# Two edits to the mixture-of-experts stage of a one-core trunk-layer kernel: the first tile's row list and the last tile's result

## What is computed

```python
def hier_moe(h, w_coarse, b_coarse, w_fine, b_fine, w_gate_up, w_down):
    ...
    combine = ((p_grp * grp_oh)[:, :, None] * within[:, None, :]).reshape(-1, N_EXPERTS)
    out = jnp.zeros_like(t)
    for e in range(N_EXPERTS):
        gg, uu = jnp.split(t @ w_gate_up[e], 2, axis=-1)
        out = out + combine[:, e:e + 1] * ((jax.nn.silu(gg) * uu) @ w_down[e])
    return out.reshape(b, s, d)
...
    x = ln_affine(DEEPNORM_ALPHA * x + g2 * y, p['ln2_g'][l], p['ln2_b'][l])
```

## Time and profile before

| | us |
|---|---|
| median of 3 runs | 1366.87 |
| lowest, highest | 1365.56, 1367.5 |
| the profiled execution, its own time | 1364.97 |
| its span, first to last instruction | 1363.0 |
| PE busy | 1237.8 (91%) |
| DVE busy | 954.3 (70%) |
| ACT busy | 657.6 (48%) |
| POOL busy | 202.1 (15%) |
| chain that ended last: PE, DVE, DMA | 79%, 9%, 5% |
| mean granted TensorE clock | 0.953 of full speed |

### The profile page before, as it was taken

The page is one execution under the profiler, slowest core; times in us unless marked ns, Lnnn a source line. Parts: engine busy times, 40 slices in busy tenths (PEclk is TensorE's granted clock), DMA queues, the critical chain, the costliest instruction groups (busy, mean ns, idle before and its releaser), DMA issues.

```text
span 1363.0 us, 20458 instructions
## 1 busy us (share of the span) xinstructions
PE 1237.8 (91%) x6673; PEld 996.4 (73%) x6673; DVE 954.3 (70%) x1716; ACT 657.6 (48%) x1049; POOL 202.1 (15%) x312
## 2 busy tenths in 40 slices
PE   7999999999999899998998999993799999999940
PEld 4777777777888788887876788773588888888830
DVE  5765531839461688888777526788799999999938
ACT  1522222223222677776763213123387788788812
POOL 0023221020232000011111001001011111111101
PEclk9899999999999899999999999995799999999975
DMA  9977664462646678743004534457899999999925
GB/s 349 288 247 239 209 224 171 155 224 83 211 144 182 169 196 217 194 128 90 25 23 132 194 110 140 152 194 266 304 323 366 372 389 385 391 383 379 332 111 146
DMA packets 150338, 301.05 MB, mean 221 GB/s; under 512 B 20380, under 2 KB 31196, under 8 KB 150264
## 3 DMA queue, kind: packets, MB, share of 16 engines
q1 hardware_dynamic: 122424, 232.72, 50.0%
q0 software_dynamic: 21920, 62.13, 14.5%
q10 hardware_dynamic: 5920, 5.24, 1.3%
HBM read 258.71 MB, written 53.38 MB: 229 GB/s over the span
## 4 chain that ended last, share of the span: by engine, by line
PE 79%; DVE 9%; DMA 5%; issue 2%; SPq 2%; ACT 1%; POOL 0%; DVEq 0%; POOLq 0%; ACTq 0%
PE psum_pair L1740 9%; PE psum_pair L1742 8%; PE psum_pair L1741 8%; PE psum_pair L1842 5%; PE psum_pair L2019 5%; PE psum_pair L2021 5%; PE psum_pair L2020 5%; PE psum_pair L1909 4%; PE psum_pair L1911 3%; PE psum_pair L1910 3%; PE psum_pair L1868 3%; PE psum_pair L1853 3%; DMA k_bundle<-k_transposed 3%; PE psum_pair L2034 3%; PE psum_pair L2036 3%; PE psum_pair L2035 3%
## 5 line engine op out<-in xcount | busy, mean ns | idle before, releaser
L1740 PE MATMUL psum_pair<-w_parts,h_hi 128*128 128x512 f32 x520 | 207.4, 399 | 3.0 <-DVE h_lo L1271 3.0
L1742 PE MATMUL psum_pair<-w_parts,h_lo 128*128 128x512 f32 x520 | 203.7, 392 | 0.0
L1741 PE MATMUL psum_pair<-w_parts,h_hi 128*128 128x512 f32 x520 | 203.3, 391 | 0.0
L1121 DVE TENSOR_TENSOR w_parts<-w_raw,w_parts 128x1024 fp32r<-128x1024 f32 x72 | 83.3, 1219 | 92.9 <-ACT w_parts L842 92.3
L982 ACT ACTIVATE p_unnormed<-psum_pair,minus_max 128x640 f32<-128x640 f32 (+1 forms) x160 | 113.3, 711 | 68.6 <-DVE minus_max L1349 67.2
L1842 PE MATMUL psum_pair<-k_bundle,q_bundle 128*128 128x512 f32 (+1 forms) x576 | 124.1, 344 | 14.0 <-ACT p_unnormed L982 9.5
L1349 DVE TENSOR_REDUCE minus_max<-psum_pair 128x1 f32<-128x640 f32 (+1 forms) x160 | 111.8, 715 | 32.3 <-PE psum_pair L1842 29.6
L1740 PEld LDWEIGHTS psum_pair<-w_parts,h_hi 128*128 128x128 f32 x520 | 98.2, 189 | 30.8 <-issue 11.6
L1842 PEld LDWEIGHTS psum_pair<-k_bundle,q_bundle 128*128 128x128 f32 x576 | 89.0, 195 | 34.6 <-issue 20.9
L1742 PEld LDWEIGHTS psum_pair<-w_parts,h_lo 128*128 128x128 f32 x520 | 98.0, 189 | 21.1
L1741 PEld LDWEIGHTS psum_pair<-w_parts,h_hi 128*128 128x128 f32 x520 | 98.3, 189 | 19.5
(11 more groups left out here) (342 smaller groups left out, 2553.5 us busy)
## 6 DMA issues: line engine op xcount, KB each, us to landing
w_raw<-in_w_gate_up SPq DMA_DIRECT2D x76, 512.0 KB, 8.6
w_raw_c<-in_w_gate_up SPq DMA_DIRECT2D x72, 512.0 KB, 9.5
w_raw_b<-in_w_down SPq DMA_DIRECT2D x72, 512.0 KB, 8.6
w_raw<-in_w_in SPq DMA_DIRECT2D x52, 512.0 KB, 8.6
ada_raw<-in_w_ada SPq DMA_DIRECT2D x32, 512.0 KB, 7.6
k_bundle<-k_transposed SPq DMA_DIRECT2D x28, 384.0 KB, 8.5
q_transposed<-turned_staging POOLq DMA_DIRECT2D x40, 256.0 KB, 6.4
ada_raw_early<-in_w_ada SPq DMA_DIRECT2D x16, 512.0 KB, 8.8
```

Of the source, the lines that this page charges most:

```text
L1121: dve.tensor_tensor(w_parts[b % 2][:, 1, c], w_raw[:, c], w_parts[b % 2][:, 0, c].bitcast(F32), ALU.subtract).then_inc(lo_done, 1)
L1740: pe.matmul(out, a_hi, hi, start=kk == 0, stop=False)
L1741: pe.matmul(out, a_hi, lo, start=False, stop=False)
L1742: return pe.matmul(out, a_lo, hi, start=False, stop=kk == KD - 1)
```

## The change

**First tile.** After `positions`, DVE also builds a one-hot matrix `first_tile_pick` for expert 0 alone (a token that chose expert 0 sits in tile 0 at its position), and PE multiplies it by the token numbers (five products with one column, on `psum_pair` 3). DVE turns the result into `rows_wanted`, and the gather of tile 0 starts from that, ahead of the table. The clearing of `expert_in` goes from DVE to ACT. PE turns tile 0 between the two halves of the table's products. ACT rounds tile 0 ahead of the split of the third block of weights; DVE takes its rest after the first chunk of block 0, and writes the table after the four chunks.

**Last tile.** Its result isn't scattered. ACT and DVE take it out of PSUM as a high and a low part, DVE builds a one-hot `last_tile_pick` from the tokens of its slots, and for each tile of tokens PE sums up first choices, second choices (by an fp32 product with the identity) and the last tile's rows (by two products with the one-hot) in PSUM; DVE's `combine` starts from there, without its addition. `moe_over` is given after the store of the last tile but one. Since rows of `pair_rows` that the last tile would have written are then read unwritten, the whole scratch is set to zero beforehand: SP writes a row of zeros to DRAM early on, and after the values of bundles 1 to 5 issues two DMAs each from that row to 128 rows of `pair_rows` (ten of 512 KB, DRAM to DRAM).

```diff
@@ SP
             weights(1)
+            sp.dma_start(zero_scr.rearrange("o (p n) -> (o p) n", p=P), zeros[:]).then_inc(out_cleared, 16)
...
                 load_v(sp, bi, v_in[bi % 2])
+                if bi == 1:
+                    sp.wait_ge(out_cleared, 16 * (TL + 1))
+                if bi <= NT:
+                    for i in (bi - 1, NT + bi - 1):
+                        sp.dma_start(pair_scr[i * P:(i + 1) * P], zero_scr[0:1, :].to_broadcast([P, D])).then_inc(out_cleared, 16)
@@ ACT
             split_hi_moe((0, 0, 0))
+            act.wait_ge(h2_done, NT)
+            act.wait_ge(ones_done, 1)
+            act.activation(xs[:].rearrange("p (k q) -> p k q", q=P), over(ones[:], 1, [P, KD, P]), ACT.Copy, scale=0.0).then_inc(xs_clear, 1)
             split_hi_moe((1, 1, 0))
+            round_x(0)
             act.wait_ge(route_done, 1)
             middle = middle_tiles(act)
             act.wait_ge(pj_ready, N_PJ2)
             split_hi_moe(gate_block(1))
-            round_x(0)
...
-            take_out(middle + 1, last_block(middle + 1)[0])
+            act.wait_ge(moe_used, used(last_block(middle + 1)[0] + 1))
+            act.wait_ge(y_free, middle + 1 + OFF)
+            act.activation(yo_hi[:], pair[3][:], ACT.Copy, scale=out_now[:, 2:3].bitcast(F32)).then_inc(y_copied, 1)
@@ DVE
+            link(dve.scalar_tensor_tensor(pri[:], mask[:, :, 0], -float(NOBODY), posn[:, 0:NT, 0], ALU.mult, ALU.add))
+            dve.scalar_tensor_tensor(first_pick[:], over(pri[:], 2, [P, NT, P]), float(NOBODY), over(places[:], 1, [P, NT, P]),
+                                     ALU.add, ALU.is_equal).then_inc(picks_done, 1)
...
+            dve.wait_ge(slots_ready, 1)
+            dve.tensor_scalar(row_now[:], pair[3][:, 0:1], -1.0, float(NOBODY), ALU.mult, ALU.add).then_inc(table_done, 1)
...
-            dve.memset(xs[:], 0.0).then_inc(xs_clear, 1)
-            dve.wait_ge(slots_ready, 1)
+            split_lo_moe((0, 0, 0), (0,))
+            rest_x(0)
+            split_lo_moe((0, 0, 0), range(1, NC_CH))
+            dve.wait_ge(slots_ready, 2)
...
-            split_lo_moe((0, 0, 0))
-            rest_x(0)
...
+            dve.wait_ge(y_free, middle + 1 + OFF)
+            for tt in range(NT):
+                link(dve.tensor_scalar(token[:, tt:tt + 1], out_now[:, 1:2], -float(tt * P), None, ALU.add))
+            link(dve.tensor_tensor(last_pick[:], over(places[:], 1, [P, NT, P]),
+                                   over(token[:], 2, [P, NT, P]), ALU.is_equal))
+            dve.wait_ge(y_copied, middle + 2 + OFF)
+            dve.scalar_tensor_tensor(yo_lo[:], pair[3][:], out_now[:, 2:3].bitcast(F32), yo_hi[:].bitcast(F32),
+                                     ALU.mult, ALU.subtract).then_inc(al_done, 1)
...
-                dve.wait_ge(y_in[tt], 32)
-                link(dve.tensor_tensor(y, y, yc[:, tt], ALU.add))
-                link(dve.tensor_tensor(y, y, g2[:, cnd], ALU.mult))
+                dve.wait_ge(sums_ready, tt + 1)
+                link(dve.tensor_tensor(y, pair[tt % 4][:], g2[:, cnd], ALU.mult))
@@ PE
+            for tt in range(NT):
+                pe.wait_ge(y_in[tt], 32)
+                if tt == 4:
+                    pe.wait_ge(z_done, 1)
+                if tt == 3:
+                    pe.wait_ge(al_done, middle + 3 + OFF)
+                for h in range(2):
+                    cols = slice(h * CW, (h + 1) * CW)
+                    pe.matmul(pair[tt % 4][:, cols], ident[:], ya[:, tt, cols], start=True, stop=False)
+                    pe.matmul(pair[tt % 4][:, cols], ident[:], yc[:, tt, cols], start=False, stop=False)
+                if tt == 0:
+                    pe.wait_ge(al_done, middle + 3 + OFF)
+                for h in range(2):
+                    cols = slice(h * CW, (h + 1) * CW)
+                    pe.matmul(pair[tt % 4][:, cols], last_pick[:, tt], yo_hi[:, cols], start=False, stop=False)
+                    last = pe.matmul(pair[tt % 4][:, cols], last_pick[:, tt], yo_lo[:, cols], start=False, stop=True)
+                last.then_inc(sums_ready, 1)
@@ POOL
+            pool.wait_ge(xs_clear, 1)
             pool.wait_ge(table_done, 1)
-            gather(table[:, 0, 1:2])
-            pool.wait_ge(table_done, 2)
+            gather(row_now[:])
+            pool.wait_ge(route_done, 1)
+            middle = middle_tiles(pool)
+            pool.wait_ge(out_cleared, 16 * (TL + 1 + 2 * NT))
+            pool.wait_ge(table_done, 3)
...
                 pool.wait_ge(y_st, 16 * (tile + 1))
+                if left == 1:
+                    pool.nop().then_inc(moe_over, 1)
...
-            pool.wait_ge(y_free, middle + 1 + OFF)
-            store_rows(middle + 1, 0)
```

More of the change, by code:

```diff
@@ L148, in hybrid_step @@
         nlam = sb("minus_lambda", [P, 1])
+        zeros = sb("zeros", [P, D // P])
         w_raw = sb("w_raw", [P, NC_CH, 2, CW])
+        s7 = ExitStack()
+        yc = sb("second_expert_rows", [P, NT, D], F32, s7)
+        yo_hi = sb("last_rows_hi", [P, D], F32R, s7)
+        yo_lo = sb("last_rows_lo", [P, D], F32R, s7)
+        s7.close()
         w_parts = [sb("w_parts0", [P, 2, NC_CH, 2, CW], F32R)]
@@ L153, in hybrid_step @@
         sx.close()
+        s8 = ExitStack()
+        ya = sb("first_expert_rows", [P, NT, D], F32, s8)
+        last_pick = sb("last_tile_pick", [P, NT, P], F32R, s8)
+        zs = sb("z_sums", [P, NT], F32, s8)
+        zm = sb("z_minus_mean", [P, NT], F32, s8)
+        zq = sb("z_squares", [P, NT], F32, s8)
+        zv = sb("z_var", [P, NT], F32, s8)
+        zr = sb("z_rstd", [P, NT], F32, s8)
+        zt = sb("z_root_step", [P, 2], F32, s8)
+        zi = sb("z_root_bits", [P, 2], I32, s8)
+        token = sb("last_tile_tokens", [P, NT], F32, s8)
+        s8.close()
         w_parts.append(sb("w_parts1", [P, 2, NC_CH, 2, CW], F32R))
@@ L1236, in _ @@
             link(dve.memset(cond_cols[:], 0.0))
+            link(dve.memset(zeros[:], 0.0))
             dve.tensor_copy(cond_cols[:, :, 0:2], cond_t[:]).then_inc(cond_silu, 1)
@@ L1596, in _, with split_lo_moe @@
                 dve.nop().then_inc(sm, OFF)
-            def split_lo_moe(block):
+            def split_lo_moe(block, chunks=range(NC_CH)):
                 q, place, _ = block
-                for c in range(NC_CH):
+                for c in chunks:
                     dve.wait_ge(hi_done, NC_CH * (NB + q) + c + 1)
@@ L1990, in _ @@
             last.then_inc(pre_done, 1)
-            for i in range(2):
-                pe.wait_ge(picks_done, i + 1)
-                for tt in range(NT):
-                    last = pe.matmul(pair[2][:, 0:3 * TILES], at_place[:, i, tt], tile_words[:, i, tt].rearrange("p w t -> p (w t)"),
-                                     start=i == 0 and tt == 0, stop=i == 1 and tt == NT - 1)
-            last.then_inc(slots_ready, 1)
             for sm in (x_turned, moe_used, aturned):
                 pe.nop().then_inc(sm, OFF)
+            pe.wait_ge(picks_done, 1)
+            for tt in range(NT):
+                last = pe.matmul(pair[3][:, 0:1], first_pick[:, tt], words[:, 0, tt, 1:2], start=tt == 0, stop=tt == NT - 1)
+            last.then_inc(slots_ready, 1)
             def turn_x(tile):
@@ L2006, in turn_x @@
                 last.then_inc(x_turned, 1)
+            for i in range(2):
+                if i:
+                    turn_x(0)
+                pe.wait_ge(picks_done, i + 2)
+                for tt in range(NT):
+                    last = pe.matmul(pair[2][:, 0:3 * TILES], at_place[:, i, tt], tile_words[:, i, tt].rearrange("p w t -> p (w t)"),
+                                     start=i == 0 and tt == 0, stop=i == 1 and tt == NT - 1)
+            last.then_inc(slots_ready, 1)
             def half_of_hidden(tile, block, r):
@@ L2247, in _ @@
             store_rows(middle, 1)
-            pool.wait_ge(y_free, middle + 1 + OFF)
-            store_rows(middle + 1, 0)
             pool.wait_ge(xs_in, 16 * (middle + 3))
-            pool.nop().then_inc(moe_over, 1)
-            pool.wait_ge(out_cleared, 16 * TL)
+            pool.nop().then_inc(pool_turn, 1)
             for tt in range(TL):
```

20 lines of the change are left out of this document (5 added, 15 removed).

## The result

The changed kernel takes **1370.53 us** (median of 20 executions, 1366.16 to 1374.35), the kernel before 1366.07 beside it (20 executions). The ratio is 1.0028 with a 95% interval of 1.0016 to 1.004: slower by 0.28%, by more than the 0.2% that the prediction takes as the line to no change. Forecast were 1363.5, faster than before, and a range from 1355.5 to 1369.5.

What follows compares the result with a forecast made beforehand. PE was taken to bound the experts' loop, with serial work at its ends and key loads limiting attention. -11.5 - 3.5 + 10.6 + 1 = -3.4 gave 1361.6 on the profiled execution, 1363.5 against the median; range 1355.5 to 1369.5.

Steps and rivals of the forecast that it cites:

- Last tile, -11.5: Tail after the experts' loop: first combine 5.6 us earlier and five DVE additions dropped (6.2 us), between -10 and -12.
- Rival 3: Tail sums: TensorE's clock stays at 1.2 GHz, the end is +6.4 instead of -11.5, 1381.4 us in all; chance 0.06.
- First tile, -3.5: Start of the experts' loop: DVE saves most of its 4.33 us wait and the 0.91 clearing, pays 1.4; between 0 and -5.
- lands at 950.2: First tile: the gather leaves at about 944.5 and lands 5.75 us later, so DVE waits only 0.3 us.
- Rival 4: First tile gives nothing: the gather lands late or DVE loses its saving elsewhere; 1367.0 us, chance 0.12.
- Fills, +10.6: Attention: pairs of zero fills ahead of the keys in SP's queue delay the bundles, +10.6 us from bundle 6 on.
- the 29.3 of the forecast: Attention: a bundle starts no earlier than 29.3 us after the one before the last, plus fills ahead of its keys.
- 4.6 us a pair: Attention: DMA cost of two 512 KB fills, priced from the bias row copy, 2.09 MB in 9.2 us at 227 GB/s.
- upper bound of 6.0: Attention: highest price taken for a pair of fills, in us, the 4.6 with 1.4 for the issue added.
- Which chain holds: Attention: bundles 3, 5, 7 get 9.2 us of fills; bundles 2, 4, 6 get 10.6, which holds from bundle 6 on.
- A slower TensorE, +1: Attention: PE's longer waits, from 1.25 to 6 us, slow its matmuls for a while; +1 us, 0 to 3.
- Rival 2: Attention: fills cost 6.0 us a pair and each wait lowers the clock, +15 and +2, so 1368.9 us; chance 0.12.

## Why the prediction was wrong

The forecast was -3.4 us; the medians give +4.5, and the spans, in which the terms can be told apart, +5.9. So the sum is off by 9.3 there, and no single step makes it: 2.6 are the first tile, 2.5 PE's waits for the keys, 2.6 the slower TensorE, 2.1 the end, 0.4 a delay that was there at bundle 3, less 0.9 that came back between bundle 7 and the positions. The waits that the prediction named are the ones that came; the prices it gave them were too low.

1. **Last tile, -11.5: right.** -11.6 measured, and here by its parts, not by luck. The first combine came 5.7 us earlier (forecast 5.6), five additions went, DVE waited 0.27 at the second tile (0.4 forecast), and the one-hot lay in DVE's wait. From the last down product's end (1329.15) to DVE's last end are 32.8 us (forecast 33). Rival 3, the clock at half in the sums, didn't come: the granted clock was 1.00 from 1330 to 1350. The Trainium skill ("TensorE: Matmul & The Clock Gate", "Part 4: PE-mode transpose") holds that a transpose on PE doesn't count as PE being busy in the same way; the products here are ordinary fp32 ones with the identity, and they kept 1.00.
2. **First tile, -3.5: the step that failed is "lands at 950.2", 5.75 us after the issue.** That price was read from a gather that left when the queues were all but empty; moved forward by 8.5 us against the positions (13.2 before, 4.7 after), it left into 4.2 MB of other loads and took 9.6. The rest of the step was right: with SP's loads away the stretch is 3.2 to 4.1 us shorter. Rival 4 named a late gather, without its cause, and got 0.12. The trace before could have told: the tail's loads go out there between 940.6 and 942.8 us and take up to 11.7 us, and the gather was to leave at 944.5.
3. **Fills, +10.6: the mechanism was right, the size was not.** PE waits for keys before bundles 3 and 5 (7.38 and 8.08 us, forecast 4 to 6), and from bundle 3 to 5 it is 37.71 us: the 29.3 of the forecast, 6.57 for the fills and 1.85 for the slower TensorE. The added waits are 13.1 us up to bundle 7. The term that was mis-sized is "4.6 us a pair": it measured 6.15 and 6.57. Where nothing waits for it a pair takes 5.4 (27 us for ten), and the mean of the earlier trace rows was already too high a rate, as its 9.2 us hold faster traffic at both ends. Inside them, from 48 to 54 us, the rate is about 204 GB/s, 5.1 us a pair:

```profile
48.00:50.00 2.00, 2.00 (x11) 1.65 (x10) 1.97 (x3) 1.51 (x4) 0.00 (x0) 1.00 1.11 205
```

Another 0.8 to 1.2 comes on top ahead of the keys, and what it consists of stays open (two issues take 1.15 us, other transfers run beside). The upper bound of 6.0 was thus too low. Which chain holds was off too: the forecast took the even bundles for the later ones, but they never waited long, since each odd bundle's delay gave their loads the time.
4. **A slower TensorE, +1: measured 1.85 and 1.79, in all 3.6**, above the bound of 3. The granted clock fell to 0.50 during each of the two long stops, and PE ran on at it for some us after. The forecast took its 1 from a stop of 2.15 us; the stops that the fills make are three to four times that.
5. **The end, not forecast: +2.1** between DVE's last end and the end of the span. The last store took 4.3 us to land (2.6 before); in the kernel before with fills it took 3.9, with the old tail, so part of this is no work of the change. In the traces of all variants this last stretch is 6.1 to 7.9 us, with the old tail (6.60) as with the new, and only in the one of the kernel before 4.8. The cause wasn't tested.

Terms in all: -11.6 - 0.9 + 16.3 + 2.1 = +5.9, from 1363.0 to 1368.9. Rival 2 with "from 6.2 us a pair the whole is slower" is what happened, at a chance of 0.12; its 1368.9 us for the whole lay 1.6 below the median. That it came so near is in part luck, as it had neither the first tile's loss nor the end's.

The prediction also weighed a page: the Trainium skill's 341 GB/s for 1 MB from HBM to SBUF ("DMA: Bandwidth & Descriptors", "Bandwidth"). It is near the copies of 128 different rows, 346 and 372 GB/s in the windows shown, though these go from DRAM to DRAM; the fills from one row, at 207, are far from it. The bias row in the trace was the better guide, since it too is one row read many times.

## What to carry to other kernels

A transfer that nobody waits for isn't free when a load that somebody waits for stands behind it in the queue: the ten fills cost 15 to 18 us ahead of the keys and nothing that shows in the two other places. Before placing one, look at what the queue issues next and who stops for that, and put it behind that load or into a stretch with idle DMA. When an edit moves a DMA forward in time, its latency is that of the traffic at the new place, not that of the old row (9.6 us here, not 5.75); look for what is under way there, and whether its user is far off, as the tail's x rows were.

## What the runs showed of the hardware

- Fills that read one 4 KB row of DRAM 128 times ran at 207 GB/s, all traffic included, ten of them in 27 us; copies of 128 different rows, same bytes and same targets, at 334 to 372 GB/s, ten in 16 us. In the place of the change that was 4.5 us of the kernel's time.
- A gather of 128 rows landed 3.3 us after issue with no loads ahead of it and 9.6 us with 4.2 MB of loads under way; without SP's 2.6 MB of these it was 3.4.
- In PE's stops of 7 to 8 us the granted clock fell to 0.50, and the next two bundles took 1.8 us more in all than before the change; after one of 4.0 us the first eight products took 2.82 us instead of 1.58 as well.
